# Two attention prologues of a five-block kernel: head rotations, filler matmuls and spread matmuls moved to other steps

## What is computed

```python
# sparse attention ("at"): 16 heads of 64, queries normed and rotated, keys of 4 groups normed and rotated
q = partial_rope(rms_norm(q, q_g), cos, sin);  k = partial_rope(rms_norm(k, k_g), cos, sin)
...
logits = where(valid, q @ k.T * scale, -inf);  o = softmax(logits) @ v
# last block ("b"): heads of kind A (normed queries and keys), heads of kind B (96 wide: 64 plain and 32 rotated)
kb = rms_norm(concat([k_nope, k_rope]), knorm_b_g);  out_b = causal softmax attention(qb, kb, vb)
```

## Time and profile before

| what | value |
|---|---|
| three executions | 1598.49, 1590.61, 1593.86 us, median 1593.86 |
| the profiled execution, own time | 1598.74 us |
| its span in the profile | 1597.0 us |
| PE busy | 1553.8 us, 97% |
| DVE, ACT, POOL busy | 661.7, 781.9, 1137.4 us |
| mean granted PE clock | 0.985 |

### The profile page before, as it was taken

How to read it: one execution, slowest core, us unless ns; L and a number is a source line. 1 busy time by engine, 2 the same in 40 slices (tenths; PEclk the granted TensorE clock), 3 DMA queues, 4 the chain that set the end, 5 groups by cost and what they waited for, 6 DMA issues and landing times.

```text
span 1597.0 us, 40790 instructions
## 1 busy us (share of the span) xinstructions
PE 1553.8 (97%) x16162; PEld 1487.6 (93%) x16162; DVE 661.7 (41%) x1615; ACT 781.9 (49%) x1297; POOL 1137.4 (71%) x848
## 2 busy tenths in 40 slices
PE   6999999989999999999999999999999999999998
PEld 6999999878899999999999987799999988799998
DVE  4334468764435333223332257643341435542200
ACT  5444557633245444454444444654445535565532
POOL 6876858973338877778777784088878974478885
PEclk9999999999889999999999999999999998999999
DMA  7544543210023544455444541065536532235552
GB/s 268 184 172 139 181 146 133 106 69 2 2 81 109 197 169 151 164 193 196 167 150 164 188 164 50 17 235 201 183 127 208 188 139 100 87 133 184 184 185 79
DMA packets 37909, 231.31 MB, mean 145 GB/s; under 512 B 4527, under 2 KB 6680, under 8 KB 16552
## 3 DMA queue, kind: packets, MB, share of 16 engines
q1 hardware_dynamic: 36552, 228.57, 41.0%
q10 hardware_dynamic: 1248, 1.24, 0.2%
HBM read 228.67 MB, written 2.63 MB: 145 GB/s over the span
## 4 chain that ended last, share of the span: by engine, by line
PE 73%; DVE 3%; issue 1%; ACT 1%; POOL 0%; DMA 0%; SPq 0%; DVEq 0%; POOLq 0%; ACTq 0%
PE PS L842 58%; PE PS L841 1%; PE PS L1101 1%; PE PS L1108 1%; PE PS L1116 1%; PE PS L1516 1%; PE PS L1146 1%; PE PS L1140 1%; PE PS L1492 0%; PE PS L1680 0%; PE PS L1668 0%; PE PS L1502 0%; PE PS L1292 0%; DMA raw<-w_f_in_in 0%; ACT whi L2740 0%
## 5 line engine op out<-in xcount | busy, mean ns | idle before, releaser
L796 POOL TENSOR_TENSOR wlo<-raw,whi 128x256 fp32r<-128x256 f32 (+1 forms) x742 | 1070.0, 1475 | 361.0 <-ACT whi L2740 339.0
L842 PE MATMUL PS<-xh,whi 128*128 128x272 f32 (+1 forms) x2304 | 666.2, 289 | 20.9 <-POOL wlo L796 16.2
L842 PE MATMUL PS<-xl,whi 128*128 128x272 f32 (+1 forms) x2304 | 657.7, 285 | 0.0
L842 PE MATMUL PS<-xh,wlo 128*128 128x272 f32 (+1 forms) x2304 | 657.1, 285 | 0.0
L2740 ACT ACTIVATE whi<-raw 128x1024 fp32r<-128x1024 f32 x468 | 455.5, 982 | 360.7 <-PE PS L842 336.5
L842 PEld LDWEIGHTS PS<-xh,whi 128*128 128x128 f32 x2304 | 433.5, 188 | 30.9 <-issue 22.6
L842 PEld LDWEIGHTS PS<-xl,whi 128*128 128x128 f32 x2304 | 434.9, 189 | 0.5
L842 PEld LDWEIGHTS PS<-xh,wlo 128*128 128x128 f32 x2304 | 435.2, 189 | 0.0
L842 PE MATMUL PS<-hid_h,whi 128*128 128x272 f32 (+1 forms) x960 | 273.7, 285 | 2.1 <-POOL wlo L796 2.1
L842 PE MATMUL PS<-hid_h,wlo 128*128 128x272 f32 (+1 forms) x960 | 273.7, 285 | 0.0
L842 PE MATMUL PS<-hid_l,whi 128*128 128x272 f32 (+1 forms) x960 | 272.8, 284 | 0.0
(11 more groups left out here) (427 smaller groups left out, 1662.8 us busy)
## 6 DMA issues: line engine op xcount, KB each, us to landing
raw<-w_f_in_in SPq DMA_DIRECT2D x88, 1024.0 KB, 4.8
raw<-w_f_dn_in SPq DMA_DIRECT2D x64, 704.0 KB, 4.1
raw<-w_b_ff_in SPq DMA_DIRECT2D x32, 1024.0 KB, 4.8
raw<-w_rk_k_in SPq DMA_DIRECT2D x4, 1024.0 KB, 4.9
raw<-w_rk_r_in SPq DMA_DIRECT2D x4, 1024.0 KB, 4.9
raw<-w_rk_v_in SPq DMA_DIRECT2D x4, 1024.0 KB, 5.4
raw<-w_rk_o_in SPq DMA_DIRECT2D x4, 1024.0 KB, 5.3
raw<-w_at_q_in SPq DMA_DIRECT2D x4, 1024.0 KB, 4.9
```

What stands on the lines that cost most here:

```text
L796: last = nc.gpsimd.tensor_tensor(wlo[U % SPL][:, piece], raw[U % RAW][:, piece], whi[U % SPL][:, piece].bitcast(F32), ALU.subtract)
L842: mm(out, a, b, start=start and n == 0, stop=stop and n == 2, **kw)
```

## The change

In the sparse attention: `query_sum(1)` and `query_sum(3)` each move one place up, so that the last sum stands ahead of the last value tile. Rotations 1 and 2 move from steps 1 and 2 to step 0, with 5 constants between them. The 6 constants of steps 3 and 5 become 3, those of step 6 go, and 5 are new in step 2, ahead of its transposes; the waits for finished rotations are kept (in steps 3, 5 and 7). DVE makes `query_cosine(2)` after the top round that it preceded.

In the last block: `b_values(0, 1)` is cut in two halves, one after the first two `hinva` pairs and one after the last two. The two key pairs move behind `attend(0)` and `attend(1)`, and DVE's two scalings of `kn` into its steps 1 and 2. As `spread` is then read after the first probabilities are written, `prnb` moves to other memory, and `krot` is placed ahead of `lgb`.

```diff
@@ sparse attention, PE
             query_rotation(0)
             query_sum(0)
+            query_sum(1)
...
             value_tile(0, PS[:, bank(G), 0:256])
-            query_sum(1)
             query_sum(2)
+            query_sum(3)
             value_tile(2, PS[:, bank(G), 256:512]).then_inc(s_part, 1)
-            query_sum(3)
...
+                if j == 2:
+                    constants(5, PS[:, bank(o0 + 1), 0:128])
                 if 0 <= j - 1 < 16:
                     head_transposes(j - 1)
                 if 0 <= j - 2 < 16:
                     head_values(j - 2)
-                if j in (1, 2, 4):
-                    if j == 4:
-                        pe.wait_ge(s_hout, 3)
-                    query_rotation({1: 1, 2: 2, 4: 3}[j])
-                if j in (3, 5, 6):
-                    pe.wait_ge(s_hout, {3: 3, 5: 4, 6: 5}[j])
-                    constants(6, PS[:, ahead + (j == 5), 0:128])
+                if j == 0:
+                    query_rotation(1)
+                    constants(5, PS[:, ahead + 1, 0:128])
+                    query_rotation(2)
+                if j == 3:
+                    pe.wait_ge(s_hout, 3)
+                    constants(3, PS[:, ahead, 0:128])
+                if j == 4:
+                    query_rotation(3)
+                if j == 5:
+                    pe.wait_ge(s_hout, 4)
+                    constants(3, PS[:, ahead + 1, 0:128])
+                if j == 7:
+                    pe.wait_ge(s_hout, 5)
@@ last block, PE
-            for n, j in enumerate((0, 4, 2, 6)):
...
+            head_spread(0)
+            head_spread(1)
+            b_values(0, 1, range(2))
+            head_spread(2)
+            head_spread(3)
+            b_values(0, 1, range(2, 4))
+            rope_spread()
             pe.wait_ge(s_hsc, AT_HSC + 2)
             scores(0)
             pe.wait_ge(s_x, X0["cq"] + 3)
             b_queries(0, 0)
             attend(0)
+            key_spread(0)
             b_queries(0, 1)
             pe.wait_ge(s_hsc, AT_HSC + 4)
             attend(1)
+            key_spread(1)
             b_queries(1, 0)
@@ DVE
             v.reciprocal(hinvk[0:4, :], hinvk[0:4, :]).then_inc(s_hinv, 1)
-            query_cosine(2)
             top_rounds(0, 1)
             top_end(0)
+            query_cosine(2)
...
+                if J in (1, 2):
+                    key_scale(J - 1)
```

More of the change, by code:

```diff
@@ L449, in build @@
         b2.here = rings + 4 * 8 * SEQ
+        prnb = Region(b2.here)("prnb", [128, 2, 2, SEQ])
         kr = b2("kr", [128, SEQ])
@@ L452, in build @@
         krs = b2("krs", [32, SEQ])
+        krot = b2("krot", [128, SEQ])
         lgb = Region(b2.here)("lgb", [128, 2, 2, SEQ])
         ksq = b2("ksq", [128, 4, SEQ])
-        krot = b2("krot", [128, SEQ])
         qn = b2("qn", [128, 4, SEQ])
@@ L488, in build @@
         spread = tb("spread", [16, 1280])
-        prnb = Region(posi_at)("prnb", [128, 2, 2, SEQ])
         ptb = tb("ptb", [128, 2, 2, SEQ])
@@ L1582, in b_pairs, with b_values @@
                         norm_sum(norm, SEQ)
-            def b_values(u, q):
+            def b_values(u, q, part=range(4)):
                 name = ("b_va", "b_vb")[u]
@@ L1589, in b_values @@
                     pe.wait_ge(s_free, G - 1)
-                for k in range(4 * q, 4 * q + 4):
+                for k in [4 * q + d for d in part]:
                     for j in range(2):
@@ L1595, in b_values @@
                                         skip_group_check=True)
-                last.then_inc(s_unit, 1)
+                if 3 in part:
+                    last.then_inc(s_unit, 1)
             def b_queries(u, q):
@@ L1759, in _, with head_spread @@
             pe.wait_ge(b_cc, 1)
-            for n, j in enumerate((0, 4, 2, 6)):
+            def head_spread(n):
+                j = (0, 4, 2, 6)[n]
                 for q in range(2):
@@ L1763, in _, with rope_spread, key_spread @@
                 last.then_inc(s_hb, 1)
[L1764 to L1769, removed]
+            def rope_spread():
+                pe.wait_ge(s_hinv, AT2 + 2)
+                for q in range(2):
+                    last = mm(PS[:, 2, q * SEQ:q * SEQ + SEQ], spread_rope(q), hinvb[:, :], start=True, stop=True)
+                last.then_inc(s_hb, 1)
+            def key_spread(n):
                 if n:
@@ L2620, in _, with key_scale @@
                             ALU.mult).then_inc(s_hsc, 1)
-            for n in range(2):
+            def key_scale(n):
                 dve.wait_ge(s_hb, AT_HB + 6 + n)
```

## The result

| | median | executions |
|---|---|---|
| before | 1596.22 us | 20 (1590.61 to 1601.75) |
| changed | 1589.61 us | 20 (1585.20 to 1595.97) |

The ratio is 0.9953, 95% interval 0.9939 to 0.9967: faster by 0.47%, which on 1596.22 is 7.5 us (5.3 to 9.7). The difference of the medians is 6.6. The three executions shown ahead of the prediction had stood 2.4 us low.

A forecast was written before the change was run, and what follows sets the result against it. PE, with 73% of the chain, was taken to bound the kernel. Sparse attention 4.9 plus last block 6.8 gave 11.7 us, less 2.4 for the median 9.3: 1584.5 us, range 1578 to 1592.

The forecast's parts named there:

- A1: Sparse attention: rotations 1 and 2 in step 0 fill PE's idle time and leave the loop, 2.82 us, PE 0.13 late.
- A2: Sparse attention: with PE occupied, the clock's fall at 984.7 should not come; scores and transposes gain 1.03 us.
- A3: Sparse attention: eleven fillers instead of eighteen, seven fewer on PE's path, 1.79 us.
- A4: Sparse attention: DVE runs about 1.6 us earlier, and PE gets a new 0.6 us wait for step 3's probabilities.
- B1: Last block: spreads split up between full-width products keep the clock at 1.00, with nothing added; 6.55 us.
- B2: Last block: key pairs moved behind `attend` have their 0.25 us wait for DVE covered.
- B3: Last block: DVE's two scalings, 0.75 us each, in steps 1 and 2 cost 0, at most 1.5 together.
- Rows, not columns: Last block: the clock answers to rows streamed, not to columns or busy time; no size of its own.
- R1: Last block: the clock falls all the same; gain 4.9 + 0.25, 1588.7 us; chance 0.17.
- R4: Last block: alternation holds PE at 1.2 GHz throughout, up to 40 us; slower, 1602.2 us; chance 0.04.
- R2: Whole kernel: timed executions mostly have short falls or none; gain about 5.6, 1588.3 us; chance 0.12.
- R3: Sparse attention: the chain turns to DVE and ACT, losing 1.79 and 0.6 us; 1586.9 us; chance 0.08.

The follow-up runs named there:

- the filled gap: The kernel before with 12 constants added where PE idles behind `head_scores(1)` of step 0; ratio to before 0.9973, sparse-attention section 27.48 us.
- full rows: The kernel before with its 14 narrow spread matmuls of the last block replaced by ones streaming 128 rows; ratio to before 0.9976, section 26.38 us.
- the probe: The kernel before with five blocks of 40 filler matmuls of different shapes ahead of the last feed-forward; last-block section 31.49 us.

## Why the prediction was right, and where it was off

The time, 1589.61, lies in the range of 1578 to 1592 but 5 us above the 1584.5; the gain that I forecast against the median was 9.3, the measured one 7.5 (5.3 to 9.7). At 0.47% it lies just short of the half per cent that I had set as the bound of "faster" (chance 0.60), so it fell, narrowly, to "the same" (0.35), though the measurement does tell it from no change.

- **A1, the rotations.** Right. They fill the wait, and `head_scores(2)` comes 3.70 us behind `head_scores(1)`, 0.23 sooner than before, where I had said 0.13 later. DVE's wait for rotation 1 is gone.
- **A2, the clock.** Right, by the filled gap (1.37 us, the same clock loss with nothing else changed) and by five profiles of the full new form of A with no fall there.
- **A3, the fillers.** Seven fewer on the path: right in the count. That the five of step 0 cost nothing is shown; that those of step 2 stand in a wait for ACT's copy is shown by the 0.93 us that come in their place (the five took 1.22). I had priced a fall of the clock in A at "1 to 1.7 us"; without fillers it cost 4.5 and 16.5.
- **A4, what is late next.** The mechanism was right: PE waits for DVE's probabilities. The size was low, 0.30 + 0.86 = 1.16 us where I took 0.6 (bounds 0 and 1.3). The reorder gave 0.48 for the 0.4.
- **A in all:** 2.82 + 1.03 + 1.79 + 0.23 - 1.16 = 4.71, measured 4.73, forecast 4.9.
- **B1, the spreads.** The cause was right, and the term for that one profile too: 6.55 forecast, 6.68 measured with full rows, 6.3 by the estimate above for the narrow ones. "Nothing is added" was wrong: at full clock the new section is 1.33 us longer. The sum for the pair was thus 5.35, not 6.8. The larger error was to read the term from a single execution. Old B's falls are 6.8 to 13.6 us long, and on the mean of four the gain is 3.8. I had taken off half of 4.9 us for this; the direction was right, and it was too little.
- **B2, B3.** The key pairs' wait is gone, and DVE's scalings in steps 1 and 2 hold nobody up: in the changed kernel PE is busy through the whole of section B.
- **Rows, not columns.** "The rows streamed, not columns" was half of it. 8 streamed columns let the clock fall in the probe as well; few rows of the result did not. The probe's expectation already names columns beside rows and calls that the prediction's theory; the prediction had rows alone. I had the sums at 1305.37, which stream 256 columns and whose narrow side, 8, is the stationary one, and took them for more than they show.
- **The rivals.** R1 (the clock falls in B all the same) and R4 (alternating work holds it down in B) did not happen in any of seven profiles of the complete new form. Something like R4 happened in A: with the fillers gone, ordinary steps of the loop stayed at 0.50 for up to 41 us. R2 holds in part: shorter falls than in the profile shown are the usual case in B, not in A. R3 did not come.

With the sections alone, A's 4.73 and B's 3.8 give 8.5, inside the interval of the measurement.

## What to carry to other kernels

A fall of the clock behind busy work is found with the granted clock beside the shapes of the timeline, not beside busy time: look for runs of matmuls that stream few rows (16 or 8 here) or few columns, and for PE's idle time, just ahead of it, and break the run up with work that has to be done anyway. Each cut costs something as well (here 0.4 to 0.5 us by estimate), so it pays only where the fall comes often. Before pricing a fall from one profile, look at several: the same instructions gave 6.8 to 13.6 us at the lower clock, while a section without a fall repeated to 0.02 us. And look at the mean clock of all executions before calling a long fall frequent or rare.

## What the runs showed of the hardware

- 40 matmuls of 128x8 streamed (80 records) took 14.8 us, 12 of them at 0.50, and 40 of 128x128 with 8 result rows took 8.9 us at 1.00. Fewer streamed columns made the block slower, fewer result rows did not.
- Once at 0.50 behind scattered waits, the attention loop stayed there with PE busy 13.39 of 13.50 us, for 13.7 and 41.0 us. The same steps ran at 1.00 from start to end in the five profiles that have the changed kernel's full set of fillers and order.
- The stretches at 0.50 in the time mix vary from execution to execution: from its first 32-row products to its norm sums the 14 profiles need 108.65 to 116.46 us, with the code unchanged there. That is 7.8 us between the extremes, where the executions of before and of the changed kernel scatter over 11 us each.
